# Gathering the tokens of four experts at once, and scattering between the last down products

## The reference

```python
h = silu(einsum('bsd,edf->bsef', x, w_gate)) * einsum('bsd,edf->bsef', x, w_up)
h = h * comb[..., None]              # comb: weights of the two chosen experts, else 0
return einsum('bsef,efd->bsd', h, w_down)
```

## Time and profile before

| | |
|---|---|
| runs | 1821.94, 1823.3, 1828.55 us; median 1823.3 |
| profiled execution | span 1824.6 us, 28274 instructions |
| PE, weight loads, DVE, ACT, POOL busy | 1816.0, 1377.6, 737.0, 314.4, 13.9 us |
| read from memory, written | 540.78 MB, 4.24 MB |

### The profile page before, as it was taken

The page is one execution under the profiler, slowest core; times in us unless marked ns, Lnnn a source line. Parts: engine busy times, 40 slices in busy tenths (PEclk is TensorE's granted clock), DMA queues, the critical chain, the costliest instruction groups (busy, mean ns, idle before and its releaser), DMA issues.

```text
span 1824.6 us, 28274 instructions
## 1 busy us (share of the span) xinstructions
PE 1816.0 (100%) x12238; PEld 1377.6 (76%) x12238; DVE 737.0 (40%) x1531; ACT 314.4 (17%) x846; POOL 13.9 (1%) x27
## 2 busy tenths in 40 slices
PE   9999999999999999999999999999999999999999
PEld 9788887899765667656597888878996666676665
DVE  3477665676202121121235675656761021221213
ACT  3123122212101111011021231222121011110110
POOL 1000000000000000000000000000000000000000
PEclk9999999999999999999999999999999999999999
DMA  9433343447899999999884342444579999999997
GB/s 385 165 139 142 147 168 141 189 163 287 341 425 424 426 428 426 427 427 421 346 356 150 133 178 112 167 177 153 200 283 358 421 425 427 426 428 427 426 422 305
DMA packets 51439, 546.92 MB, mean 300 GB/s; under 512 B 5872, under 2 KB 6000, under 8 KB 14576
## 3 DMA queue, kind: packets, MB, share of 16 engines
q1 hardware_dynamic: 48816, 531.47, 71.1%
q0 software_dynamic: 2496, 13.57, 2.0%
HBM read 540.78 MB, written 4.24 MB: 299 GB/s over the span
## 4 chain that ended last, share of the span: by engine, by line
PE 99%; DMA 0%; issue 0%; DVE 0%; SPq 0%; DVEq 0%
PE ps L833 96%; PE ps L887 1%; PE ps L1191 1%; PE ps L1299 1%; PE ps L903 0%; PE ps L895 0%; DMA ring<-in_w_lat 0%; PE ps L1358 0%; PE ps L986 0%; DVE ring L1892 0%; PE ps L1072 0%; PE ps L1099 0%; PE ps L1138 0%; DVE X L1921 0%; DVE X L2131 0%
## 5 line engine op out<-in xcount | busy, mean ns | idle before, releaser
L833 PE MATMUL ps<-ring,scr 128*64 128x256 f32 (+2 forms) x3488 | 624.6, 423 | 0.1
L833 PEld LDWEIGHTS ps<-ring,scr 128*64 128x64 f32 (+1 forms) x3488 | 336.9, 138 | 212.7 <-issue 119.3
L833 PE MATMUL ps<-ring,XN 128*128 128x256 f32 (+2 forms) x1184 | 242.2, 361 | 1.2 <-DMA ring<-in_w_lat 1.2
L833 PEld LDWEIGHTS ps<-ring,XN 128*128 128x128 f32 x1184 | 210.7, 190 | 21.7 <-issue 2.3
L833 PE MATMUL ps<-ring,X 128*128 128x256 f32 x896 | 200.6, 379 | 0.0
L833 PE MATMUL ps<-XN,ring 128*128 128x128 f32 (+1 forms) x1312 | 195.8, 306 | 0.0
L833 PEld LDWEIGHTS ps<-XN,ring 128*128 128x128 f32 x1312 | 180.2, 191 | 12.7 <-issue 3.1
L833 PEld LDWEIGHTS ps<-ring,X 128*128 128x128 f32 x896 | 169.6, 190 | 22.7
L833 PE MATMUL ps<-PR,scr 128*64 128x256 f32 (+2 forms) x704 | 173.8, 402 | 0.0
L2167 DVE TENSOR_TENSOR v_mla<-scr,ps 128x256 f32<-128x256 f32 x32 | 13.5, 421 | 390.6 <-PE ps L833 390.6
L833 PE MATMUL ps<-BIAS,scr 128*64 128x256 f32 (+1 forms) x608 | 157.2, 414 | 0.0
(11 more groups left out here) (276 smaller groups left out, 1454.7 us busy)
## 6 DMA issues: line engine op xcount, KB each, us to landing
ring<-in_moe_w_gate SPq DMA_DIRECT2D x38, 2048.0 KB, 20.2
ring<-in_w_main SPq DMA_DIRECT2D x36, 2048.0 KB, 9.5
ring<-in_moe_w_down SPq DMA_DIRECT2D x32, 2048.0 KB, 22.2
ring<-in_moe_w_up SPq DMA_DIRECT2D x30, 2048.0 KB, 17.3
ring<-in_w_out_a SPq DMA_DIRECT2D x16, 1280.0 KB, 6.0
PR<-in_moe_w_up SPq DMA_DIRECT2D x10, 2048.0 KB, 16.3
XN<-in_moe_w_down SPq DMA_DIRECT2D x10, 2048.0 KB, 19.2
ring<-in_moe_w_up SPq DMA_DIRECT2D x20, 1024.0 KB, 21.5
```

Source lines behind the costliest of these rows:

```text
L833: return pe.matmul(o, lhsT, rhs, start=start, stop=stop, skip_group_check=True)
```

## The change

The capacity is counted by halves of the tokens: each expert has 32 places for each half of 128 tokens instead of 64 for all. Four experts (a quad) then fill 128 columns for each half, and one gather serves four experts. The halves have columns of their own, so nothing is accumulated over them. A gather comes in eight parts of two feature tiles. Quad 0 is gathered in the head; quads 1 to 3 in pairs 1, 3 and 5, parts 0 to 3 ahead of u1 and parts 4 to 7 behind it. The gathered tokens of four experts need twice the room, which is lent from other buffers (homes). The flag for the sweep is set if an expert has more than 32 tokens in one half. In the head, ACT evicts parts 0, 1, 2, 4, 6 and DVE parts 3, 5, 7; later ACT evicts all eight.

The down weights lie in memory by runs of 256 columns, each with all four k. In the last pair dy3 is cut into two halves of 256 columns (dy3, dy4), the last block of down weights comes in a half and two quarters, and six of the eight scatters stand between the down products, with their adds on DVE between its copies. Two scatters, and the scaled copies for the next layer, stay behind the branch. The sweep's own code is adapted and left out here, as are the bank planner's entries.

```diff
+CAP_T = CAP // NT
+QUAD = 4
+N_QUAD = NE // QUAD
+PARTS = KT // 2
...
+def gathered_in(i):
+
+    return (i + 1) // 2 if i % 2 and i + 1 < NE // 2 else None
+
+
+def plan_homes():
+
+    homes = [{(k, p): p * KT + k for k in range(KT) for p in range(2)}]
+    for q in range(1, N_QUAD):
+        left = [[homes[-1][k, p] for k in range(KT)] for p in range(2)]
+        homes.append({(k, p): left[k // (KT // 2)][2 * (k % (KT // 2)) + p] for k in range(KT) for p in range(2)})
+    return homes
...
-        XG = scr[:, 1024:1024 + KT * 2 * CAP].rearrange("p (k n) -> p k n", k=KT)
+        nf = neg_all[:, :, :].rearrange("p d s -> p (d s)")
+        bf = BIAS[:, :, :].rearrange("p h n -> p (h n)")
+        homes = [scr[:, 1024 + n * P:1024 + (n + 1) * P] for n in range(KT)]
+        homes += [prf[:, at + 1024 + SLOT + n * P:at + 1024 + SLOT + (n + 1) * P] for n in range(8)]
+        homes += [bf[:, SLOT + n * P:SLOT + (n + 1) * P] for n in range(4)]
+        homes += [nf[:, n * P:(n + 1) * P] for n in range(4)]
+
+        def xg(k, i):
+
+            return homes[HOMES[i // 2][k, i % 2]]
...
-                    for half in range(2):
+                    for lo, hi in ((0, 2), (2, 4)) if n != "dn1" else ((0, 2), (2, 3), (3, 4)):
                         for j in range(2):
                             name = f"{n}{j}_{NE // 2 - 1}"
-                            if half == 0:
+                            if lo == 0:
                                 sp.wait_ge(*empty(name, l))
-                            part = slice(half * (SLOT // 2), (half + 1) * (SLOT // 2))
+                            part = slice(lo * (SLOT // 4), hi * (SLOT // 4))
                             sp.dma_start(slot(name)[:, part], w[j][:, part]).then_inc(
-                                halves_in[f"{n}{j}"] if half == 0 else slot_full[SLOTS.where(name)], 16)
+                                halves_in[f"{n}{j}"] if lo == 0 else slot_full[SLOTS.where(name)] if hi == 4 else third_in[j], 16)
...
-                pe.wait_ge(*freed("rank", l))
                 pe.wait_ge(*after("picked", l))
-                o = bank("rank")
-                mm(o[:, 0:NE], tri, picked[:, 0, 0:NE])
-                mm(o[:, NE:2 * NE], ones[:, :], picked[:, 0, 0:NE], True, False)
-                mm(o[:, NE:2 * NE], tri, picked[:, 1, 0:NE], False, True).then_inc(*made("rank"))
-                pe.wait_ge(*freed("count", l))
-                mm(bank("count")[:, 0:NE], ones[:, :], picked[:, 0, 0:NE], True, False)
-                mm(bank("count")[:, 0:NE], ones[:, :], picked[:, 1, 0:NE], False, True).then_inc(*made("count"))
+                for name, w in (("rank", tri), ("count", ones[:, :])):
+                    pe.wait_ge(*freed(name, l))
+                    for t in range(NT):
+                        last = mm(bank(name)[:, t * NE:(t + 1) * NE], w, picked[:, t, 0:NE])
+                    last.then_inc(*made(name))
                 by_token(TOKENS_LATE[-1])
 
-                def gather(i, ns=range(4)):
+                def gather(quad, ns):
 
                     for n in ns:
-                        name = f"gx{n}_{i}"
+                        name = f"gx{n}_{quad}"
                         pe.wait_ge(*freed(name, l))
                         for t in range(NT):
                             if n == 0:
-                                pe.wait_ge(*after("gm", l, NT * i + t))
-                            for k in range(4):
-                                d = (4 * n + k) * P
-                                last = mm(bank(name)[:, k * 2 * CAP:(k + 1) * 2 * CAP], xtok[:, t, d:d + P], Gm[:, t, :], t == 0 and k == 0, t == NT - 1)
+                                pe.wait_ge(*after("gm", l, NT * quad + t))
+                            if quad == 0 and n % 2 == 0:
+                                pe.wait_ge(*copied(f"xt{t * (KT // 4) + n // 2}", l))
+                            for q in range(2):
+                                d = (2 * n + q) * P
+                                last = mm(bank(name)[:, q * S + t * P:q * S + (t + 1) * P], xtok[:, t, d:d + P], Gm[:, t, :])
                         last.then_inc(*made(name))
...
-                        if n == "g0":
-                            pe.wait_ge(*copied(f"gx{q}_{i}", l))
                         for k in range(4 * q, 4 * q + 4):
+                            if n == "g0" and i % 2 == 0 and k % 2 == 0:
+                                pe.wait_ge(*copied(f"gx{k // 2}_{i // 2}", l))
                             for j in range(2):
                                 own_rows = slice(j * CAP, (j + 1) * CAP)
-                                last = mm(bank(name)[own_rows, 0:CH], XG[:, k, own_rows], w[j][:, k, :], k == 0, k == KT - 1)
+                                last = mm(bank(name)[own_rows, 0:CH], xg(k, i)[:, own_rows], w[j][:, k, :], k == 0, k == KT - 1)
...
-                for j in range(NT * KT // 4 - 1):
-                    pe.wait_ge(*copied(f"xt{j}", l))
                 gather(0, (0, 1))
                 for q in range(4):
+                    if q < 3:
+                        gather(0, (2 * q + 2, 2 * q + 3))
                     expert("g0", 0, (q,))
                     expert("u0", 0, (q,))
-                    if q == 1:
-                        pe.wait_ge(*copied(f"xt{NT * KT // 4 - 1}", l))
-                    if q < 2:
-                        gather(0, (q + 2,))
...
-                    elif i:
-                        gather(i + 1)
+                    elif gathered_in(i):
+                        gather(gathered_in(i), range(PARTS // 2))
                     expert("u1", i)
+                    if gathered_in(i):
+                        gather(gathered_in(i), range(PARTS // 2, PARTS))
                     if i == 0:
-                        gather(1, (0,))
                         turn_h(1, 0)
-                        gather(1, (1,))
...
+                    def down(name, half, lo, hi):
+
+                        w = [slot(f"dn{half}{j}_{i}").rearrange("p (n k c) -> p n k c", n=4, k=4) for j in range(2)]
+                        pe.wait_ge(*freed(name, l))
+                        for k in range(4):
+                            for j in range(2):
+                                own_rows = slice(j * CAP, (j + 1) * CAP)
+                                last = mm(bank(name)[own_rows, 0:(hi - lo) * CH], hs[:, k, own_rows], w[j][:, lo:hi, k, :], k == 0, k == 3)
+                        last.then_inc(*made(name))
+
+                    def last_blocks(half):
+                        for j in range(2):
+                            pe.wait_ge(*loaded(f"dn{half}{j}_{i}", l))
+
+                    if i == NE // 2 - 1:
+                        for j in range(2):
+                            block_in(f"dn0{j}_{i}")
+                        down(f"dy0_{i}", 0, 0, 2)
+                        last_blocks(0)
+                        down(f"dy1_{i}", 0, 2, 4)
+                        pe.wait_ge(*copied(f"sw_{i}", l))
+                        pe.wait_ge(*copied(f"dy0_{i}", l))
+                        scatter(i, (0, 1))
+                        for j in range(2):
+                            block_in(f"dn1{j}_{i}")
+                        down(f"dy2_{i}", 1, 0, 2)
+                        pe.wait_ge(*copied(f"dy1_{i}", l))
+                        scatter(i, (2, 3))
+                        for j in range(2):
+                            pe.wait_ge(third_in[j], 16 * (l + 1))
+                        down(f"dy3_{i}", 1, 2, 3)
+                        pe.wait_ge(*copied(f"dy2_{i}", l))
+                        scatter(i, (4, 5))
+                        last_blocks(1)
+                        down(f"dy4_{i}", 1, 3, 4)
+                        break
...
-                pe.wait_ge(*copied(f"sw_{NE // 2 - 1}", l))
-                for n in range(4):
+                for n in (3, 4):
                     pe.wait_ge(*copied(f"dy{n}_{NE // 2 - 1}", l))
-                    scatter(NE // 2 - 1, (2 * n, 2 * n + 1))
+                    scatter(NE // 2 - 1, (n + 3,))
...
+                def tokens_of_quad(quad):
                     for t in range(NT):
-                        ins = dve.tensor_scalar(o[:, t, :], iota, rank[:, t, e:e + 1], w[:, t, e:e + 1], ALU.is_equal, ALU.mult)
-                    return ins
-
-                def tokens_of_pair(i):
-                    for t in range(NT):
-                        for j in range(2):
-                            e = 2 * i + j
-                            ins = dve.tensor_scalar(Gm[:, t, j * CAP:(j + 1) * CAP], iota, rank[:, t, e:e + 1], seen[:, t, e:e + 1], ALU.is_equal, ALU.mult)
+                        for j in range(QUAD):
+                            ins = one_hot(Gm[:, t, j * CAP_T:(j + 1) * CAP_T], t, QUAD * quad + j, seen)
                         ins.then_inc(*signal("gm"))
...
-                for n in (1, 3):
-                    gathered(f"gx{n}_0", n, l)
+                own.did(dve.memset(Gw, 0.0))
+                for n in (3, 5, 7):
+                    gathered(n, l)
```

(77 more changed lines are left out.)

54 lines of the change are left out of this document (19 added, 35 removed).

## The result

Timed side by side, the changed kernel takes 1830.26 us in the median of five runs (1829.16 to 1832.69), the one before 1822.99 (1821.94 to 1828.55). The ratio is 1.0029, interval 1.0018 to 1.0040. A second timing later gave 1.0036 (1.0023 to 1.0048). The forecast was 1821.3 us with a range up to 1828: wrong in sign, and some 9 us too low. The change of 7.3 us is less than the 0.5% set as the mark, but clear of the noise.

What follows compares the result with a forecast made beforehand. PE and the weight DMA both limit it, so only work behind the last binding landing or ahead of the stream counts: 1.8 + 0.8 - 0.6 = 2.0 us off, giving 1821.3 us; range 1813 to 1828, own range 1819.7 to 1824.4.

Steps and rivals of the forecast that it cites:

- The stream in the middle: Experts' middle: weight stream takes 58.9 us a pair against PE's 56.72, so removing 30 us of gather a layer gains nothing.
- The head: First gather of each layer: eight narrower one-hots delay it, 0.5 us in layer 1, 0.1 in layer 0; -0.6 us (0 to -1.5).
- The branch's stall: Layer ends, PE's branch round the sweep: 3.7 us gain less the stall, 1.8 us in layer 0, 0 in layer 1.
- What is late next: End of layer 0: DVE's copies and branch stall, taken as 0.8 us, limit the gain to 1.8 us (0.4 to 2.6).
- The base: Whole kernel: profiled span 1824.6 us becomes 1822.6; the median of the runs, 1823.3, lies 1.3 below the profiled span.
- The clock did fall where PE waits: Rival: PE's waits lower the clock behind the last binding landing, 7 us added, 1828; chance 0.13.
- the sign that the prediction set for this rival: Clock rival, behind the landing near 873: a clock near 0.5 there would show it; 2.0 us a layer decides.
- the Trainium skill's rule of the prediction: Matmul bursts parted by DMA waits: each wait lowers the clock, making the clock rival likeliest, 1828 or more.
- The stream did not start earlier: Rival, start of the experts: pieces released sooner move the weight stream up, at most 5.6 us a layer, 1810; chance 0.12.
- the sweep did not run: Rival: an expert exceeds 32 tokens in a half and the sweep's branch is taken, 470 us; chance 0.01.

Runs made afterwards that it cites:

- second trace of before: The kernel before, unchanged, run and traced again: ratio 0.9998, median 1824.7 us on this chip, span 1822.9.
- the second trace: The changed kernel, unedited, run and traced again beside the follow-up kernels: ratio 1.0036 to the kernel before.
- the gather alone with its last product narrow: Gather by four with the old order of the last pair, dy3 made as two runs of 256 columns, against the kernel before: ratio 1.0035.

## Why the prediction was wrong

*The stream in the middle: right.* Gather halved, span hardly helped, PE's idle time in its place, the landing at 873.0 against 873.3, the down product at 891.68 against 891.7. In layer 1 it started at 1798.16, 1.1 us ahead of the 1799.3 forecast.

*The head: right in size.* First gather to first gate product takes 4.14 us after and 3.74 in the second trace of before, 0.4 more a layer against 0.6 for both. The gather now stands 0.36 us at its start, in both layers:

```profile
457.58 4.17 PE L872 MATMUL ps<-v_mla,PR 128*128 128x128 f32 x32 [0.36 <-issue]
```

*The branch's stall: the step that failed.* The prediction wrote "PE alone would gain 3.7 us less that stall (0 in layer 1, 1.8 in layer 0)" and carried both values over as if the stall belonged to the place. It is a difference: a jump of 3.3 to 5.8 us less the work issued ahead of it, and the change halved that work by cutting the last product into quarters. In layer 1 the term was 0 and measured 2.4 us, with 1.5 us more for the lower clock behind it: dn0 to add 7 took 26.8 us, not 22.1. In layer 0 it was 1.8 and measured 2.5 and, in the second trace, 4.1; the next layer's first matmul came at 916.19, not at 914.9, and in the second trace at 919.32. That the stall of the earlier trace rows was 1.82 us in one layer and none in the other should have been the warning: both had the same code, so one of them was just hidden (by the table 5.10 and 3.31 us of branch, over 3.4 us of work). A smaller term of the same sum was short too: from the first down product to the end of dy4 PE took 20.2 us, not 19.6, as dy3 in two narrow products takes 1.9 us twice where it took 3.4.

*What is late next: wrong engine.* The prediction made DVE's copies and its branch the limit. In layer 1 DVE stood 3.72 us waiting for PE. In layer 0 its own stall, taken as 0.8 us, was 1.74, and its last scaled copy ended at 917.73; PE went on without a break into the next layer from 916.19, so it held nothing up.

*The base.* The forecast was set against a span of 1824.6 as if it stood 1.3 above the median. The listed runs of the change are 1.8 us longer than their spans, so that profile was a run of about 1826.4, 3.4 above the median; part of it was the 5.10 us branch. The gains were counted from there.

*The rivals.* The clock did fall where PE waits: 0.83 in 690 to 700, and similar windows in every kernel that gathers by four, none in those by pairs. As far as the traces show, it cost time only where it fell into the last pair (1780 to 1790 above) or behind a stall, and there the sign that the prediction set for this rival did come: 0.55 in 1820.7 to 1824.3, 1.5 us of the loss. But it came behind the branch's stall in one layer, not from waits for weights, and it is gone without the branch, so the 1828 given for that rival was near the result mostly for another reason. By the Trainium skill's rule of the prediction, page "TensorE: Matmul & The Clock Gate", section "HAM oscillation — how this bites in real kernels", each wait would bring the clock down. Here the clock was below 1.00 in three windows of ten us in the change's experts; the waits of that page's example, 3 to 5 us, are longer than these, of 2.7 us at most in layer 0. The stream did not start earlier, and the sweep did not run.

The stages add up to 4.5 us against the second trace of before: ends +5.7, experts -3.1, fronts +1.9, of which 0.8 is the head and the rest is within what fronts vary. The ratio says 3.3 to 7.3.

## What to carry to other kernels

Where two engines bind alike, ask for each term whether it stands behind the last landing that counts; the rest of a saving comes back as waiting. A taken branch costs its fetch less the work already issued, so look at what the change leaves in the queue ahead of it: the width of the last few instructions can be worth more than their order. If a branch must be taken, put it where its engine waits for something else.

## What the runs showed of the hardware

- The branch on PE took 3.3 to 6.2 us at the layers' ends, in most traces below 4.5; in pairs 6 and 7, with the weights streaming, 5.9 to 6.2 every time. The second branch right behind it there, whose body is run, took 0.08 us.
- Of PE's work, 14 to 19 matmul records, each with its weight load, started behind the issue of the branch at a layer's end. The Trainium skill, page "TensorE: Matmul & The Clock Gate", section "Architectural detail: the array is 16× 32×32, not 1× 128×128", gives TensorE a queue of 64; with two instructions a record these runs show 28 to 38. What sets their number is not shown: in the kernel before, PE's sequencer had waited for the last weights until 903.5 and 1810.6, and issued the branch 0.2 to 0.3 us behind that.
- A second stall of 0.5 to 2.9 us can follow a taken branch when the code behind it reaches the next block of 16 KB: 0.51 us in layer 0 of the kernel before and 0.99 in its second trace, 2.88 in the gather alone with its last product narrow, each time with an instruction fetch that by the raw records ended 1.4 to 1.5 us before PE went on.
- Behind a stall of the branch the granted clock can fall to its lower level: 0.55 in 1820.7 to 1824.3, behind 2.4 us. Behind 2.5 us in layer 0 of the same trace it stayed at 1.00.
